# Expert gate and up products with the weights held in the array and 96 token rows streamed

## What is computed

```python
D_MODEL = 1024; N_EXPERTS = 16; EC_FACTOR = 2; D_EXPERT = 2 * D_MODEL
cap = max(1, EC_FACTOR * n // N_EXPERTS)          # 32 (prompt) and 64 (sample)
gates, idx = lax.top_k(aff.T, cap)
xe = xt[idx]
a = jnp.einsum('ecd,edf->ecf', xe, w_gate)
u = jnp.einsum('ecd,edf->ecf', xe, w_up)
ye = jnp.einsum('ecf,efd->ecd', jax.nn.silu(a) * u, w_down)
ye = ye * gates[..., None]
out = jnp.zeros((n, D), jnp.float32).at[idx.reshape(-1)].add(ye.reshape(-1, D))
```

## Time and profile before

| | |
|---|---|
| median of three runs | 1541.59 us |
| the profiled execution | 1541.64 us |
| its span, first to last instruction | 1539.8 us |
| mean granted TensorE clock | 0.995 of 2.4 GHz |
| PE busy | 1503.8 us, 98%, 7293 matmuls |
| PEld busy | 1228.2 us, 80%, 7293 loads |
| DVE busy | 1242.6 us, 81% |
| ACT busy | 1089.9 us, 71% |
| POOL busy | 123.3 us, 8% |
| HBM over the span | 290 GB/s |

### The profile page before, as it was taken

One profiled execution on the slowest core, in us unless ns is written; L12 is line 12 of the kernel. 1 busy time (PEld: TensorE's weight loads), 2 busy tenths in 40 slices (PEclk: granted clock), 3 DMA queues, 4 the chain that ended last, 5 costly groups with the idle time before them and its releaser, 6 DMA issues.

```text
span 1539.8 us, 18601 instructions
## 1 busy us (share of the span) xinstructions
PE 1503.8 (98%) x7293; PEld 1228.2 (80%) x7293; DVE 1242.6 (81%) x1133; ACT 1089.9 (71%) x1230; POOL 123.3 (8%) x103
## 2 busy tenths in 40 slices
PE   7999999999989999999999999999999999999997
PEld 6787777678868888888888888888888888888885
DVE  5348678785589898888889888888988888898985
ACT  7456356775457778787777878778777878778784
POOL 1023131000000101000000000010000101000000
PEclk9999999999999999999999999999999999999999
DMA  6111101401759999999999999999999999999992
GB/s 232 56 55 56 38 18 56 152 28 56 273 182 390 367 385 378 395 381 393 376 386 387 376 394 379 393 380 385 384 377 393 379 394 379 387 389 382 393 370 66
DMA packets 191942, 447.98 MB, mean 291 GB/s; under 512 B 12968, under 2 KB 13296, under 8 KB 191856
## 3 DMA queue, kind: packets, MB, share of 16 engines
q1 hardware_dynamic: 187440, 433.03, 75.3%
q0 software_dynamic: 3968, 12.65, 3.5%
q10 hardware_dynamic: 448, 1.12, 0.2%
HBM read 434.19 MB, written 12.58 MB: 290 GB/s over the span
## 4 chain that ended last, share of the span: by engine, by line
PE 89%; DVE 5%; ACT 3%; issue 1%; DMA 1%; POOLq 0%; POOL 0%; SPq 0%; ACTq 0%; DVEq 0%
PE ps L920 23%; PE ps L922 23%; PE ps L921 23%; PE ps L593 5%; PE ps L595 4%; PE ps L594 4%; PE ps L955 1%; PE ps L809 1%; PE ps L843 1%; DVE states L1456 1%; DVE slice_low L1370 1%; PE ps L913 1%; DMA slice_raw<-in_w_in 1%; ACT yr L1071 1%; DVE t L1487 1%
## 5 line engine op out<-in xcount | busy, mean ns | idle before, releaser
L1781 DVE TENSOR_TENSOR wl<-raw,wh 128x2048 fp32r<-128x2048 f32 x384 | 873.5, 2291 | 125.5 <-ACT wh L1305 123.8
L1305 ACT CAST wh<-raw 128x2048 fp32r<-128x2048 f32 x384 | 731.2, 1913 | 125.0 <-PE ps L922 122.8
L920 PE MATMUL ps<-wh,XTh 128*128 128x512 f32 x1024 | 405.4, 396 | 0.9 <-issue 0.9
L922 PE MATMUL ps<-wl,XTh 128*128 128x512 f32 x1024 | 400.0, 391 | 0.0
L921 PE MATMUL ps<-wh,XTl 128*128 128x512 f32 x1024 | 399.1, 390 | 0.0
L922 PEld LDWEIGHTS ps<-wl,XTh 128*128 128x128 f32 x1024 | 192.3, 188 | 41.0
L920 PEld LDWEIGHTS ps<-wh,XTh 128*128 128x128 f32 x1024 | 192.4, 188 | 38.8 <-issue 1.1
L921 PEld LDWEIGHTS ps<-wh,XTl 128*128 128x128 f32 x1024 | 192.6, 188 | 38.0
L920 PE MATMUL ps<-wh,gTh 128*128 128x512 f32 x512 | 201.1, 393 | 1.2 <-DVE gTl L1792 1.2
L922 PE MATMUL ps<-wl,gTh 128*128 128x512 f32 x512 | 199.7, 390 | 0.0
L921 PE MATMUL ps<-wh,gTl 128*128 128x512 f32 x512 | 199.4, 389 | 0.0
(11 more groups left out here) (244 smaller groups left out, 1553.6 us busy)
## 6 DMA issues: line engine op xcount, KB each, us to landing
raw<-in_w_gate SPq DMA_DIRECT2D x128, 1024.0 KB, 10.5
raw<-in_w_up SPq DMA_DIRECT2D x128, 1024.0 KB, 10.5
raw<-in_w_down SPq DMA_DIRECT2D x128, 1024.0 KB, 10.6
slice_raw<-in_w_in SPq DMA_DIRECT2D x6, 2048.0 KB, 8.0
X<-in_x_sample SPq DMA_DIRECT2D x8, 512.0 KB, 12.2
slice_raw<-in_w_out SPq DMA_DIRECT2D x2, 2048.0 KB, 9.2
X<-in_x_prompt SPq DMA_DIRECT2D x4, 512.0 KB, 4.4
h_rows<-hn SPq DMA_DIRECT2D x4, 512.0 KB, 3.3
```

The costliest lines, as they stand in the source:

```text
L920: pe.matmul(out, hi, rhs_h, start=first, stop=False)
L922: return pe.matmul(out, hi, rhs_l, start=False, stop=last)
L1305: act.copy(wh[:, n % CONV, :], raw[:, n % RAW, :]).then_inc(s_wh, 1)
L1781: dve.tensor_tensor(wl[:, n % CONV, :], raw[:, n % RAW, :], wh[:, n % CONV, :].bitcast(F32), ALU.subtract).then_inc(s_wl, 1)
```

## The change

In gate and up the operands trade places. The weights are held, in blocks of 128 by 128, and the 96 token rows are streamed past them. A tile has 4 blocks of the input dimension by 4 blocks (`FC`) of the section's width, and each takes three matmuls of 96 columns. The result comes out turned: 128 partitions of the inner width by 4 x 96. So `hid` is 128 by 384, and `turn_hidden` goes. ACT and DVE split `hid` directly, into two sets of `gTh` and `gTl` in place of one. The down products are as before. For the last section ACT and DVE split `hid` one tile earlier. `add_rows` takes its two waits in the other order, and POOL clears the spare columns of both sets.

```diff
-        gTh = at("gTh", 180224, [P, FC, P], F32R)
-        gTl = at("gTl", 182272, [P, FC, P], F32R)
-        hid = at("hid", 184320, [P, FS])
+        gTh = [at("gTh0", 180224, [P, FC, P], F32R), at("gTh1", 186368, [P, FC, P], F32R)]
+        gTl = [at("gTl0", 182272, [P, FC, P], F32R), at("gTl1", 200704, [P, FC, P], F32R)]
+        hid = at("hid", 184320, [P, FC, CAP])
...
             def add_rows(e):
+                if e >= 1:
+                    pool.wait_ge(s_add, 32 * e)
                 pool.wait_ge(s_y, 2 * (e + 1))
                 if e == NE - 1:
                     pool.wait_ge(s_ylast, 2)
-                if e >= 1:
-                    pool.wait_ge(s_add, 32 * e)
...
-            pool.memset(gTh[:, :, CAP:P].bitcast(F32), 0.0)
-            pool.memset(gTl[:, :, CAP:P].bitcast(F32), 0.0).then_inc(s_pad, 1)
+            for j in range(2):
+                pool.memset(gTh[j][:, :, CAP:P].bitcast(F32), 0.0)
+                pool.memset(gTl[j][:, :, CAP:P].bitcast(F32), 0.0).then_inc(s_pad, 1)
...
                     for k in range(4):
                         kk = 4 * part_ + k
-                        mm = products(ps[:, b, :], (XTh[j][:, kk, :], XTl[j][:, kk, :]),
-                                      h_[:, k, :], l_[:, k, :], kk == 0, kk == KD - 1)
+                        rows_h, rows_l = XTh[j][:, kk, 0:CAP], XTl[j][:, kk, 0:CAP]
+                        for f in range(FC):
+                            out = ps[:, b, f * CAP:(f + 1) * CAP]
+                            held_h, held_l = h_[:, k, f * P:(f + 1) * P], l_[:, k, f * P:(f + 1) * P]
+                            pe.matmul(out, held_h, rows_h, start=(kk, f) == (0, 0), stop=False)
+                            pe.matmul(out, held_h, rows_l, start=False, stop=False)
+                            mm = pe.matmul(out, held_l, rows_h, start=False, stop=(kk, f) == (KD - 1, FC - 1))
...
-            def turn_hidden(q):
-                pe.wait_ge(s_hid, q + 1)
-                if q >= 1:
-                    pe.wait_ge(s_gtl, q)
-                for f in range(FC):
-                    mm = pe.transpose(ps[:, 6, f * CAP:(f + 1) * CAP], hid[0:CAP, f * P:(f + 1) * P],
-                                      ident[0:CAP, 0:CAP])
-                mm.then_inc(s_hT, 1)
...
                 use_tile(place["g", q, 1])
-                if q >= 1:
-                    turn_hidden(q - 1)
...
             def turned(q):
-                act.wait_ge(s_hT, q + 1)
-                act.copy(gTh[:, :, 0:CAP], ps[:, 6, 0:FC * CAP].rearrange("p (f c) -> p f c", f=FC)).then_inc(s_gth, 1)
+                act.wait_ge(s_hid, q + 1)
+                if q >= 2:
+                    act.wait_ge(*tile_used("d", q - 2))
+                act.copy(gTh[q % 2][:, :, 0:CAP], hid[:]).then_inc(s_gth, 1)
...
-                    act.wait_ge(*tile_used("u", TILES[n - 1][1]))
-                    act.activation(hid[0:CAP], ps[0:CAP, TILES[n - 1][1] % 2, :], ACT.Silu).then_inc(s_silu, 1)
+                    qq = TILES[n - 1][1]
+                    act.wait_ge(*tile_used("u", qq))
+                    if qq >= 1:
+                        act.wait_ge(s_gtl, qq)
+                    act.activation(hid[:].rearrange("p f c -> p (f c)"), ps[:, qq % 2, 0:FC * CAP], ACT.Silu)\
+                        .then_inc(s_silu, 1)
...
-                if n == place["d", NQ - 1, 0]:
+                if n == place["d", NQ - 2, 1]:
                     turned(NQ - 1)
```

More of the change, by code:

```diff
@@ L942, in use_tile @@
                         d = slice(half * 512, (half + 1) * 512)
-                        mm = products(ps[:, 4 + half, :], (gTh[:, ff, :], gTl[:, ff, :]),
+                        mm = products(ps[:, 4 + half, :], (gTh[q % 2][:, ff, :], gTl[q % 2][:, ff, :]),
                                       h_[:, f, d], l_[:, f, d], s == 0 and ff == 0,
@@ L967, in _ @@
             turn_rows(0, 1)
-            pe.wait_ge(s_pad, 2)
+            pe.wait_ge(s_pad, 3)
             for q in range(NQ):
@@ L989, in _ @@
                     down(q - 1)
-            turn_hidden(NQ - 1)
             down(NQ - 1)
@@ L1791, in turned @@
                 dve.wait_ge(s_gth, q + 1)
-                dve.tensor_tensor(gTl[:, :, 0:CAP], ps[:, 6, 0:FC * CAP].rearrange("p (f c) -> p f c", f=FC),
-                                  gTh[:, :, 0:CAP].bitcast(F32), ALU.subtract).then_inc(s_gtl, 1)
+                dve.tensor_tensor(gTl[q % 2][:, :, 0:CAP], hid[:], gTh[q % 2][:, :, 0:CAP].bitcast(F32),
+                                  ALU.subtract).then_inc(s_gtl, 1)
             dve.wait_ge(s_issued, 1)
@@ L1809, in _ @@
                     dve.wait_ge(s_silu, qq + 1)
-                    dve.tensor_tensor(hid[0:CAP], hid[0:CAP], ps[0:CAP, 2 + qq % 2, :], ALU.mult)\
-                        .then_inc(s_hid, 1)
-                if n == place["d", NQ - 1, 0]:
+                    flat = hid[:].rearrange("p f c -> p (f c)")
+                    dve.tensor_tensor(flat, flat, ps[:, 2 + qq % 2, 0:FC * CAP], ALU.mult).then_inc(s_hid, 1)
+                if n == place["d", NQ - 2, 1]:
                     turned(NQ - 1)
```

## The result

The changed kernel takes 3257.2 us (median of four runs, 3250.1 to 3266.1), against 1541.67 us before: a ratio of 2.113, 95% interval 2.110 to 2.116. The direction was forecast; 2197 us and the range to 2320 us were not met. The time lies between the two values given for the rival in which the clock falls, 2870 and 3535 us.

The account below looks back on a forecast made before the run. The prediction took TensorE's matmul issue as the bound: 1541.64 us, +680 for more loads in gate and up, -24 for the turns, -1 for the end, gives 2197 us; range 2165 to 2320 us.

Parts of the forecast that it names:

- the rival in which the clock falls: Gate and up drop to 1.2 GHz: 3535 us if all tiles do, 2870 us if half; chance 0.11.
- What bounds the kernel: Experts' stage: paced by how fast TensorE issues matmuls, 0.227 us for 512 streamed columns.
- The pitch of short matmuls: Gate and up: the load sets 0.112 us a matmul, 5.38 us a tile for 2.72, +680 us.
- That the clock stays: Gate and up: the clock was expected to stay at 1.00 in the changed kernel.
- The turns: Turns of the hidden rows go: 0.37 us a set, 64 sets, -24 us.
- The end: Last section: TensorE no longer stands for the turns' copies, as ACT and DVE split `hid` earlier; -1.3 us.
- The range: 2165 to 2320 us, from pitches of 0.110 to 0.120 us and 0.3% for waits, leaving out the rivals.
- Edits at no cost: Silu, product, splits, memsets and reordered waits: costed at nothing, ACT and DVE work covered by the 26.9 us section.
- fp32r under 256 columns: Rival, gate and up: short fp32r runs as two passes, about 3575 us, or unoverlapped, about 2725 us; chance 0.05 together.
- Loads are not skipped for a repeated block and don't come cheaper: Rival on gate and up loads: a pitch of 0.082 us, or second equal loads skipped, gives about 1829 us; chance 0.025.

Follow-up runs that it names:

- E9: E1 with 8 matmuls of 512 columns put into the pause ahead of the first gate tile; 2193.4 us, ratio 1.423.
- E6: The kernel before, token rows held, with gate and up weights streamed in pieces of 256 columns, 24 matmuls a tile; 1580.1 us, ratio 1.025.
- E7: The kernel before, making only one of the four turns of the hidden rows from the second section on; 1528.6 us, ratio 0.992.
- E2: The kernel before, token rows held, with gate and up weights streamed in pieces of 128 columns, 48 matmuls a tile; 2213.0 us, ratio 1.435.
- E8: The kernel before, with the last section's turns between the last-but-one section's two down tiles and two sets of gTh and gTl; 1540.35 us, ratio 0.9990.
- E1: The changed kernel, but gate and up stream 128 columns (96 rows and 32 zero columns) in place of 96; 2232.2 us, ratio 1.448.
- E3: The changed kernel plus one discarded 512-column matmul before each 12 short ones of gate and up, from the second section on; 2462.2 us, ratio 1.597.
- E4: The changed kernel plus one discarded 512-column matmul before each 6 short ones of gate and up, from the second section on; 2698.8 us, ratio 1.751.

## Why the prediction was wrong

- **What bounds the kernel**: right. TensorE paces the stage before and after, and its count of loads decides.
- **The pitch of short matmuls**: 0.112 us was forecast and is measured wherever the clock is full, at 96 columns and at 128. Taking the price from the router's 16 and the attention's 128 columns held.
- **That the clock stays**: this is the step that failed. The forecast was priced for a clock of 1.00; it is 0.60, and that costs 3257 - 2193 = 1064 us (E9, the same count of matmuls at the full level), as much as the whole miss of 1060. The mechanism stood among the rivals, with a chance of 0.11 and with its own reason (43 ns of 112). Its price of 3535 us assumed the low level in all of gate and up; it was granted for four fifths of the stage, since each pair of down tiles restores the full level and the next gate tile begins with it. The pitch at the low level is 0.213 and not the 0.221 of the earlier trace rows, which are matmuls of 256 columns; at the full level too these take more, 0.119 (E6).
- **Why the chance was too low**: three pieces of evidence were overrated. The stretches with short matmuls at a clock of 1.00 were 1.8 us long and stood beside long matmuls; the changed kernel too holds 1.00 for 3.5 us behind its down tiles, and so such a row can't speak for 21 us. The one fall before was put down to idle time; here the clock falls with TensorE busy for 2700 of 2700 us. And the rule of the Trainium skill ("TensorE: Matmul & The Clock Gate", section "HAM oscillation") that ties falls of thin kernels to waits for data was taken to excuse a stream without waits. No run here bears that reading out.
- **The turns**: -24 us was forecast. E7 gives 13.1 for the 15.5 expected of three quarters, so about -20. E2 against E9, which differ by the turns, the end and the filling, agrees: 2213.0 - 2193.4 + 0.9 = 20.5 us for turns and end together, where 25 was forecast.
- **The end**: -1.3 us, confirmed by E8.
- **The range**: its upper end does not follow from its own terms. 2295 us and 0.3% are 2302, not 2320. Nothing hangs on it here, since 3257 lies beyond both.
- **Edits at no cost**: ACT and DVE fall to 33% and 38% busy, in the experts' stage TensorE has no row of waiting for either.
- **The other rivals**: fp32r under 256 columns stays one matmul of one pitch, as the count of 16253 and the 0.112 us show. Loads are not skipped for a repeated block and don't come cheaper.

## What to carry to other kernels

Which operand is held decides how many loads there are and how many columns stream for each; count both. Each load of 128 by 128 float32 took 0.112 us here when columns were few, as long as streaming some 250 columns; at 256 columns the pitch was still 6 ns above the streaming. Where this cover is missing, a kernel can pay twice: once for the loads, as all versions here with 96 or 128 columns do, and again for a lower clock, as the one with 96 does, though the profile calls TensorE busy all the time. Look at the granted clock in a stretch as long as the one that the change makes; and when it has fallen, try wider streaming, even of zeros, before anything else, since it may cost nothing. It gives back the clock and not the loads: E9 is still 652 us slower than the kernel before, so the better choice is the operand order that streams 512 columns for each load.

## What the runs showed of the hardware that was not expected

- The clock falls without idle time: 0.60 over 2700 us in which PE is busy for 2700, with 96 columns for each load; at 128 columns it is 1.00 (E1 from 531 us on, E2, E9).
- At the low level a load-bound matmul costs 0.213 us and not 0.112: a load is recorded with 330 ns and not 190.
- The same stream can last at either level: that of 128 columns ran at the low level for 82 us in E1, until matmuls of 512 columns in a row raised it, and at the full level in E9. The filling of E3 and E4 held the full level behind the first down tiles, and left the clock at 0.50 for over 40 us ahead of them.
- Work that computes nothing makes the changed kernel faster: 1008 more matmuls of 512 columns take it from 3257 to 2462 us.
